# Stick-breaking attention of the odd layer: values mixed in two passes of split weights, weights kept in PSUM

## What is computed

```python
def stick_breaking(q, k, v):
    """Strictly causal stick-breaking attention over 128-query blocks. (B,L,H,d) -> (B,L,H,d)."""
    ...
        z = jnp.einsum('bqhd,bkhd->bhqk', q[:, s:e], k[:, :e]).astype(jnp.float32) * scale
        ...
        log_1m = jnp.where(mask, jax.nn.log_sigmoid(-z), 0.0)
        rest = lax.cumsum(log_1m, axis=3, reverse=True) - log_1m
        a = jnp.where(mask, jnp.exp(jax.nn.log_sigmoid(z) + rest), 0.0)
        outs.append(jnp.einsum('bhqk,bkhd->bqhd', a.astype(v.dtype), v[:, :e]))
```

## Time and profile before

| what | value |
|---|---|
| time, median of 3 runs | 2318.66 us (2314.61 to 2318.88) |
| the profiled execution: time | 2321.87 us |
| its span (first to last instruction) | 2320.1 us |
| mean granted TensorE clock | 0.979 of full speed |
| PE busy | 2230.5 us, 96% of the span |
| DVE busy, ACT busy | 1118.0 us (48%), 971.5 us (42%) |
| odd stage in the trace | about 1590 to 1885 us |

### The profile page before, as it was taken

One profiled execution on the slowest core, in us unless ns is written; L12 is line 12 of the kernel. 1 busy time (PEld: TensorE's weight loads), 2 busy tenths in 40 slices (PEclk: granted clock), 3 DMA queues, 4 the chain that ended last, 5 costly groups with the idle time before them and its releaser, 6 DMA issues. The chain is left out here.

```text
span 2320.1 us, 35416 instructions
## 1 busy us (share of the span) xinstructions
PE 2230.5 (96%) x14804; PEld 1979.7 (85%) x14804; DVE 1118.0 (48%) x1677; ACT 971.5 (42%) x1411; POOL 621.3 (27%) x480
## 2 busy tenths in 40 slices
PE   7999999998999999998999999999999999999998
PEld 5887578886589987886899999999988989988987
DVE  2348625557452234896444424444555534433443
ACT  5336644356534435335433313334555533322322
POOL 2012320113213424336123302322333212310321
PEclk9999999999999989989999999999999989999999
DMA  5442023210122212130233233222111013324322
GB/s 177 138 134 62 2 73 102 91 56 5 37 79 92 73 47 73 53 114 1 58 97 92 75 102 107 80 76 91 37 55 55 19 55 91 91 78 113 91 81 74
DMA packets 235215, 175.64 MB, mean 76 GB/s; under 512 B 7732, under 2 KB 230060, under 8 KB 234544
## 3 DMA queue, kind: packets, MB, share of 16 engines
q1 hardware_dynamic: 235056, 173.37, 25.0%
HBM read 171.20 MB, written 10.09 MB: 78 GB/s over the span
## 5 line engine op out<-in xcount | busy, mean ns | idle before, releaser
L334 DVE TENSOR_TENSOR panel_lo<-panel_raw,panel_hi 128x2048 fp32r<-128x2048 f32 (+2 forms) x148 | 325.6, 2200 | 280.9 <-ACT panel_hi L326 280.9
L326 ACT ACTIVATE panel_hi<-panel_raw 128x2048 fp32r<-128x2048 f32 (+2 forms) x151 | 268.3, 1777 | 370.9 <-PE product L432 256.6
L432 PE MATMUL product<-scaled_hi,panel_hi 128*128 128x272 f32 (+2 forms) x1232 | 282.4, 299 | 2.6 <-PEq L488 1.4
L432 PE MATMUL product<-scaled_lo,panel_hi 128*128 128x272 f32 (+2 forms) x1232 | 283.0, 299 | 0.0
L432 PE MATMUL product<-scaled_hi,panel_lo 128*128 128x272 f32 (+2 forms) x1232 | 282.8, 299 | 0.0
L432 PEld LDWEIGHTS product<-scaled_hi,panel_hi 128*128 128x128 f32 x1232 | 196.5, 188 | 11.8 <-issue 2.9
L432 PEld LDWEIGHTS product<-scaled_hi,panel_lo 128*128 128x128 f32 x1232 | 195.4, 188 | 7.5
L432 PEld LDWEIGHTS product<-scaled_lo,panel_hi 128*128 128x128 f32 x1232 | 194.5, 188 | 6.7
L445 PE MATMUL product_banks<-panel_hi,scaled_hi 128*128 128x256 f32 x696 | 193.8, 278 | 0.0
L445 PE MATMUL product_banks<-panel_lo,scaled_hi 128*128 128x256 f32 x696 | 193.7, 278 | 0.0
L445 PE MATMUL product_banks<-panel_hi,scaled_lo 128*128 128x256 f32 x696 | 193.6, 278 | 0.0
(11 more groups left out here) (584 smaller groups left out, 5437.3 us busy)
## 6 DMA issues: line engine op xcount, KB each, us to landing
panel_raw<-in_w_in_dram SPq DMA_DIRECT2D x26, 1024.0 KB, 5.3
panel_raw<-in_ffn_w_gate_dram SPq DMA_DIRECT2D x44, 512.0 KB, 4.0
panel_raw<-in_ffn_w_up_dram SPq DMA_DIRECT2D x44, 512.0 KB, 5.3
panel_raw<-in_ffn_w_down_dram SPq DMA_DIRECT2D x32, 704.0 KB, 4.7
panel_raw<-in_even_w_in_dram SPq DMA_DIRECT2D x21, 1024.0 KB, 5.2
panel_raw<-in_odd_w_in_dram SPq DMA_DIRECT2D x12, 1024.0 KB, 5.2
panel_raw<-in_w_out_dram SPq DMA_DIRECT2D x8, 1024.0 KB, 6.4
panel_raw<-in_even_w_out_dram SPq DMA_DIRECT2D x8, 768.0 KB, 4.9
```

The source lines that it names most:

```text
L326: act.activation(c.hi[g % 2][:, 0:used], c.raw[g % 2][:, 0:used], ACT.Copy).then_inc(c.hi_made.sem, 1)
L334: dve.tensor_tensor(c.lo[g % 2][:, 0:used], c.raw[g % 2][:, 0:used], c.hi[g % 2][:, 0:used].bitcast(F32), ALU.subtract).then_inc(c.lo_made ...
L432: done = pe.matmul(banks[b], weight(w, k), a[:, k, u:v], start=(k == 0 and x == 0), stop=(k == chunks - 1 and x == 2))
```

## The change

The mix becomes a product of split operands. `v` now holds for each head 64 high and 64 low columns side by side, both F32R, so one matmul has 128 columns of values; the weights are split into a high and a low part, so `mix` is two passes of 128x128 matmuls, and its result lies in both halves of the 128 rows, which have to be added. The exponential writes its weights back into `z` in PSUM; ACT copies the high part into `plus_hi[h % 2]` and DVE subtracts for the low part into `plus_lo[h % 2]` (the tiles that held the sums for `add_up`). So `score(h + 2)`, which overwrites `z`, waits for `stick_lo` of head h instead of its exponential, and the `plus_hi` of head h + 2 waits for `mix(h)`. Values get a second step on DVE (`scalar_tensor_tensor`, the low half), on which `v_taken` now hangs. `half_result` on ACT copies one half of the mixed rows, and `result` on DVE adds the other and splits the sum.

The order changes too. `mix(h)` moves from iteration h + 1 (between `add_up(h + 1, 1)` and the tile behind it) to the end of iteration h, behind `score(h + 2)`; for h = 0, 4, 8 and 12 it stands at the very start of iteration h + 1. The slots are now FIRST, REST, SCORE, MIX, and in iterations with three tiles it is the slot behind `score` that is empty.

```diff
-    AFTER_FIRST, AFTER_REST, AFTER_MIX, AFTER_SCORE = range(4)
+    AFTER_FIRST, AFTER_REST, AFTER_SCORE, AFTER_MIX = range(4)
...
-            for slot in (AFTER_FIRST, AFTER_REST, AFTER_MIX, AFTER_SCORE):
-                if slot != AFTER_REST or h == GROUP * group - 3:
+            for slot in (AFTER_FIRST, AFTER_REST, AFTER_SCORE, AFTER_MIX):
+                if slot != AFTER_SCORE or h == GROUP * group - 3:
...
-        v = [c.sb(f"v{j}", [P, NB2, 256], into=stage) for j in range(2)]
+        v = [c.sb(f"v{j}", [P, NB2, GROUP, P], F32R, into=stage) for j in range(2)]
-        weight = [c.sb(f"stick{j}", [P, Stick.WIDE], into=stage) for j in range(2)]
...
+        def mixed_behind(h):
+            return 0 <= h < H - 2 and h % GROUP == 0
+
+        def mixed_at_once(h):
+            return 0 <= h < H - 2 and h % GROUP > 0
...
                 def last_exp(h, part):
                     act.wait_ge(c.rest_ready.sem, c.rest_ready.at(2 * h + part + 1))
-                    act.activation(Stick.of(weight[h % 2], part), Stick.banks(z[h % 2], part), ACT.Exp,
-                                   scale=0.125).then_inc(c.stick_made.sem, 1)
+                    act.activation(weight_of(h, part), weight_of(h, part), ACT.Exp, scale=0.125).then_inc(c.stick_made.sem, 1)
+                    act.wait_ge(c.stick_made.sem, c.stick_made.at(2 * h + part + 1))
+                    act.activation(weight_hi_of(h, part), weight_of(h, part), ACT.Copy).then_inc(c.stick_hi.sem, 1)
+
+                def half_result(h):
+                    act.wait_ge(c.mixed.sem, c.mixed.at(h + 1))
+                    act.activation(summed_of(h), mixed[other_rows_of(h), :], ACT.Copy).then_inc(c.y_half.sem, 1)
...
                             act.wait_ge(c.plus_made.sem, c.plus_made.at(2 * new + part + 1))
+                            if new >= 2:
+                                act.wait_ge(c.mixed.sem, c.mixed.at(new - 1))
                             act.activation(Stick.of(plus_hi[new % 2], part), Stick.of(x, part), ACT.Copy).then_inc(c.plus_hi.sem, 1)
+                    if mixed_at_once(h):
+                        half_result(h)
...
                 def result(h):
-                    dve.wait_ge(c.mixed.sem, c.mixed.at(h + 1))
-                    dve.tensor_copy(y_of(0, h), mixed[rows_of(h), :]).then_inc(c.y_hi.sem, 1)
+                    y = summed_of(h)
+                    dve.wait_ge(c.y_half.sem, c.y_half.at(h + 1))
+                    dve.tensor_tensor(y, mixed[rows_of(h), :], y, ALU.add).then_inc(c.y_sum.sem, 1)
+                    dve.wait_ge(c.y_sum.sem, c.y_sum.at(h + 1))
+                    dve.tensor_copy(y_of(0, h), y).then_inc(c.y_hi.sem, 1)
                     dve.wait_ge(c.y_hi.sem, c.y_hi.at(h + 1))
-                    dve.tensor_tensor(y_of(1, h), mixed[rows_of(h), :], y_of(0, h).bitcast(F32), ALU.subtract).then_inc(c.y_lo.sem, 1)
+                    dve.tensor_tensor(y_of(1, h), y, y_of(0, h).bitcast(F32), ALU.subtract).then_inc(c.y_lo.sem, 1)
+
+                def weight_low(h, part):
+                    dve.wait_ge(c.stick_hi.sem, c.stick_hi.at(2 * h + part + 1))
+                    dve.tensor_tensor(weight_lo_of(h, part), weight_of(h, part), weight_hi_of(h, part).bitcast(F32),
+                                      ALU.subtract).then_inc(c.stick_lo.sem, 1)
...
                 for h in range(-2, H):
+                    if mixed_behind(h - 1):
+                        result(h - 1)
+                    if h >= 0:
+                        weight_low(h, 0)
                     take_all(h, AFTER_FIRST)
...
+                    if h >= 0:
+                        weight_low(h, 1)
                     if h > -2 and panel_behind(h - 1) is not None:
                         panels.lo(dve, panel_behind(h - 1))
                     take_all(h, AFTER_REST)
-                    if h >= 1:
-                        result(h - 1)
-                    take_all(h, AFTER_MIX)
...
+                    if mixed_at_once(h):
+                        result(h)
...
                     for part in range(2):
-                        pe.wait_ge(c.stick_made.sem, c.stick_made.at(2 * (h - 2) + part + 1))
+                        pe.wait_ge(c.stick_lo.sem, c.stick_lo.at(2 * (h - 2) + part + 1))
...
                 def mix(h):
-                    pe.wait_ge(c.stick_made.sem, c.stick_made.at(2 * h + 2))
+                    pe.wait_ge(c.stick_lo.sem, c.stick_lo.at(2 * h + 2))
                     pe.wait_ge(c.v_taken.sem, c.v_taken.at(NB2 * (h // GROUP + 1)))
...
-                        pe.matmul(mixed[rows_of(h), u - META:], value[:, t, head], weight[h % 2][:, at:at + TOK - u],
-                                  start=(t == 0), stop=(t == NB2 - 1), skip_group_check=True)
+                        for n, x in enumerate(weights):
+                            pe.matmul(mixed[:, u - META:], value[:, t, :], x[:, at:at + TOK - u],
+                                      start=(t == 0 and n == 0), stop=(t == NB2 - 1 and n == 1), skip_group_check=True)
...
                 for h in range(-2, H):
+                    if mixed_behind(h - 1):
+                        mix(h - 1)
                     if h >= 0:
                         add_up(h, 0)
                     run_all(h, AFTER_FIRST)
+                    if h == H - 1:
+                        mix(H - 2)
                     if h >= 0:
                         add_up(h, 1)
                     run_all(h, AFTER_REST)
-                    if h >= 1:
-                        mix(h - 1)
-                    run_all(h, AFTER_MIX)
                     if h + 2 < H:
                         score(h + 2)
                     run_all(h, AFTER_SCORE)
+                    if mixed_at_once(h):
+                        mix(h)
+                    run_all(h, AFTER_MIX)
                 mix(H - 1)
```

91 lines of the change are left out of this document (74 added, 17 removed).

## The result

The changed kernel took 2385.32 us (median of 4 runs, 2381.85 to 2387.86), beside 2318.77 us for the kernel before in its 4 runs. The ratio is 1.0277, with a 95% interval from 1.0260 to 1.0294. The profiled execution took 2382.86 us with a span of 2381.1. The forecast of 2368 had the direction and the place right and was 17 us short. The time lies in the range of 2342 to 2390, at the upper edge of the inner one (2352 to 2385).

A forecast was written before the change was run, and what follows sets the result against it. PE, busy 96%, was taken to set the pace. Waits of 13.9 us less 3.2 saved per group gave 32 over three groups; start 4, end 5 and clock 8 made 49 on 2318.7: 2368 us, range 2342 to 2390.

The forecast's parts named there:

- the inner one: Range of 2352 to 2385 us, given 71%, with the panel and take waits as worked out and clock 0 to 16.
- The saving on PE: Each mix takes 1.76 us instead of 2.57, 0.81 less per head, 13 us over 16 heads.
- Step 1: In iterations 2 to 12, even ones, the tile behind add_up(h, 1) waits 2.2 us for the previous tile's take.
- Step 2: In iterations 3, 7 and 11 the value panel's low part waits for both exponentials; PE waits 6.8 us each time.
- Step 3: Smaller waits: mix(4g) for its low values, 1.7 us; takes behind a panel's low part in iterations 1, 5, 9, 1.0.
- At the start of the stage: score(2) loses the tile before it, 3 us, and mix(0) waits 1, together 4 us.
- at its end: No tiles hide the chain before mix(15), longer results and score(15)'s wait; 5 us after three savings.
- The clock: Four long PE waits each bring 1.2 GHz afterwards, 2 us each, 8 in all, bounds 0 and 20.
- The rival of 2395: Clock stays at 1.2 GHz: 5 us more lost behind each 6.8 us wait, and the stage's end; 8%.
- More slack: Queues have more slack than worked out: waits shrink by half and the clock doesn't fall, about 2340 us; 12%.
- Faster: Panel's low part ready before tile 34 and result later than the take, so those waits vanish: 2311 us; 6%.
- The four-pass rule: True float32 takes four passes, so two would halve the mix's 2.57 us, saving 20.5 us; 2303 with no wait.

The follow-up runs named there:

- run 5: Changed kernel with DVE making the result from the head's own rows, without ACT's copy, DVE's sum and the values' low half in results; 2360.21 us, ratio 1.0181.
- Run 9: Changed kernel with DVE instead of GpSimd making the second low part of each sum; 2383.20 us, ratio 1.0269.
- Run 3: Changed kernel with a panel's low part ahead of the low weights of part 1 on DVE; 2387.92 us, ratio 1.0288.
- run 2: Changed kernel with matmuls that add zeros to the next head's sums where PE would wait behind add_up(h, 1); 2372.67 us, ratio 1.0230.
- run 1: Kernel before, in its own order, with the mix in two passes of rounded weights and values, low parts left out; 2310.85 us, ratio 0.9964.
- tuned_quiet2: Changed kernel with its queues reordered and zero matmuls in three places where PE still waits; 2339.36 us, ratio 1.0089.
- take_first: Changed kernel with DVE's first take and low panel ahead of result and low weights, and ACT's take ahead of its exponentials; 2373.43 us, ratio 1.0232.

## Why the prediction was right, and what was mis-sized

**The saving on PE.** Predicted 1.76 us per mix and 0.81 saved; measured 1.74 and 0.83. The neighbouring pairs of `add_up` were the right price.

**Step 1, the tile behind `add_up(h, 1)`.** The mechanism was right, and run 5 shows it. The size was too small: three waits of 3.6 and three of 2.8 where 2.2 was predicted, 19.3 us and not 13.2 (the other 1.8 us of the 21.1 are short waits of 0.3). The step that was off is the price of DVE's work on the result: the copy, put at 0.4 with 0.69 as its upper end, took 1.01, and in iterations 2, 6 and 10 the subtraction behind it took 1.8 instead of 0.69. Run 9 shows that both come from GpSimd's work beside them.

**Step 2, the panel.** Predicted E + 12.4 and 6.8 us, three times; measured E + 12.42 and 6.7. All ten links are in series. Run 3 takes one of them out and the wait falls by 1.7.

**Step 3.** The mix behind the last value tile waited 1.6, predicted 1.7. The take in iterations 1, 5 and 9 waited 0.3 to 0.4, predicted 1.0. At the start of the stage 2 us were added where I had put 4, at its end 8.6 where I had put 7.4 (5 and three savings). In sum 55 us of waits were added, and 53 predicted (13.9 three times, 4 and 7.4). That the sum came so close is partly luck: what step 1 has too little, step 3 and the start have too much.

**The clock.** This is the term that failed. I took 2 us for each of four long waits, 8 in all, with 0 and 20 as bounds; the rest column gives 23 us, more than the upper bound, and run 2 takes 20 of them away with zero matmuls. I had reasoned that dense tiles follow the waits, so the clock would come back as after 1623.57. What I missed is that half clock came to other places as well: to the end of the stage, at 0.50 to 0.67 for 40 us, and to stretches with waits of 2.8 to 3.6 us only (0.68 and 0.74 in the windows of 1670 and 1760), which I had priced at nothing. The rival of 2395 had this mechanism for the panel waits and the end; the time lies between it and the forecast.

**The other rivals.** "More slack" fell with step 2's 6.7 us. "Faster" had its kernel in run 1: without the new order the two passes win 8.5 us. The four-pass rule that I named beside it would have given 20.5 us of saving, and the mixes show 13.3. That kernel leaves out the weights' low parts and can't simply be completed: ACT's high and DVE's low weights need a place while the sums of the next head but one are written, and in the changed kernel they share the tiles of these sums, which forces each mix ahead of them. Whether another layout of SBUF gives that room wasn't tried. The best kernel that does all the work, `tuned_quiet2`, stays 0.9% above the kernel before. Its stage is 19.5 us longer: 16.2 of waits, 12.3 of zero matmuls in what were waits, and 4.3 of the clock, less the 13.3 saved. 8 of the 16 are at the end of the stage.

## What to carry to other kernels

Where one engine is 96% busy, look up what stands in the shadow of the work that you shorten or move, and follow each queue link by link; that gave the waits here within 2 us in sum, though single ones were off by up to 1.4. Then count what the waits do to the clock: many short ones held it down for as long as a few long ones, and cost more, since PE works through them; sum up the time at half clock per stage and look whether PE is busy in it. And ask of any time won on PE what it will wait for next, before counting it.

## What the runs showed of the hardware

- **Short waits hold TensorE's clock down.** In `take_first`, with 32 waits of 1.4 us on average and none above 3.3 in the stage save the last (3.7), it stood at 1.2 GHz for 96 of 356 us. The last waits ahead of the window below were one of 1.13 us, which ended at 1645.81, and one of 1.46 us, which ended at 1657.91. PE is full of work in it, at a mean clock of 0.70:

```profile
1660.00:1670.00 10.00, 10.00 (x60) 9.91 (x60) 1.50 (x2) 3.46 (x5) 2.62 (x2) 0.70 0.01 2
```

  Matmuls of zeros in the waits (filler) kept it at 2.4 GHz, so what they multiply didn't matter here. The Trainium skill says of frequent micro-idles between groups of matmuls that the clock swings between its levels ("TensorE: Matmul & The Clock Gate", A second HAM failure mode); take_first agrees.
- **Of DVE and GpSimd, the one that starts second stands still, where both read SBUF.** In iteration 6, GpSimd made `plus_lo` from 1753.69 to 1755.72 and `k_low` from 1756.01 to 1757.30 (the first two rows), and beside them DVE's copy took 1.01 and its subtraction 1.81 us, which start at 1754.99 and 1756.04. The sum at 1754.26, which reads one operand from PSUM, kept its 0.69:

```profile
1753.69 2.03 POOL L3606 TENSOR_TENSOR plus_lo<-soft,plus_hi 128x864 fp32r<-128x864 f32 x1 [7.97 <-ACT plus_hi L3446]
1756.01 1.29 POOL L3584 TENSOR_TENSOR k_low<-k,k_twice 64x528 fp32r<-64x528 f32 x1 [0.29 <-ACT k_twice L3377]
```

```profile
1754.26 0.69 DVE L3478 TENSOR_TENSOR k<-stick_mixed,k 64x512 f32<-64x512 f32 x1 [1.00 <-ACT k L3387]
1754.99 1.01 DVE L3480 CAST q_hi<-k 64x512 fp32r<-64x512 f32 x1
1756.04 1.81 DVE L3482 TENSOR_TENSOR q_lo<-k,q_hi 64x512 fp32r<-64x512 f32 x1
```

  The copy ended 0.28 us behind GpSimd's `plus_lo` and the subtraction 0.55 us behind `k_low`, each 0.14 less than it takes alone (0.42 and 0.69). With half the bandwidth each, an estimate from these durations, they would have ended at about 1755.8 and 1757.4, not at 1756.00 and 1757.85. The Trainium skill ("SBUF — State Buffer", SBUF: two separate sides) says that "the shared pair is an **exclusive lock**, not a bandwidth split". The trace agrees, and for the subtraction it is the order of starts that decides. In iteration 6 `k_low` started 0.03 us ahead of it. In iteration 1 the subtraction started first and kept its 0.68, and `k_low` took 1.64 instead of 1.29:

```profile
1646.31 0.68 DVE L3482 TENSOR_TENSOR q_lo<-k,q_hi 64x512 fp32r<-64x512 f32 x1
1646.53 1.64 POOL L3584 TENSOR_TENSOR k_low<-k,k_twice 64x528 fp32r<-64x528 f32 x1 [0.53 <-ACT k_twice L3377]
```

  In run 9 the copy ends earlier, so in iterations 2, 6 and 10 the subtraction starts 0.08 us ahead of `k_low` and takes 0.69, while `k_low` takes 1.76.
- **An exponential in place in PSUM costs what one to SBUF costs**: in the rows above 0.58 and 0.87 us for 512 and 864 columns, as in the earlier trace rows.
